# The router of a sparse layer, computed from the unscaled input while the last output tiles still run

## The reference, cut to what matters

```
x = x + gt1 * (mixed @ w_out)
h = rms_norm(x, g_ffn) * (1 + sc2) + sh2
g_logits = h @ w_rg + b_rg                      # 4 groups
e_all    = h @ w_re[g] + b_re                   # 4 experts in each group
g_star = argmax(g_logits);  p_sel = softmax(g_logits)[g_star]
top_v, top_i = top_k(e_all[g_star], 2);  top_w = softmax(top_v) * p_sel
y = sum over the two experts e of  top_w[e] * (silu(h @ w_gate[e]) * (h @ w_up[e])) @ w_down[e]
x = x + gt2 * y
```

## Time and profile before

| what | us |
|---|---|
| three runs: median (lowest to highest) | 2783.74 (2782.13 to 2788.76) |
| the profiled execution, device time | 2782.57 |
| its span, first to last instruction | 2780.7 |
| PE busy, of the span | 2687.7 (97%) |
| DVE busy | 1986.5 (71%) |
| ACT busy | 1456.6 (52%) |
| mean granted TensorE clock, share of full speed | 0.986 |

### The profile page before, as it was taken

One profiled execution on the slowest core, in us unless ns is written; L12 is line 12 of the kernel. 1 busy time (PEld: TensorE's weight loads), 2 busy tenths in 40 slices (PEclk: granted clock), 3 DMA queues, 4 the chain that ended last, 5 costly groups with the idle time before them and its releaser, 6 DMA issues.

```text
span 2780.7 us, 45770 instructions
## 1 busy us (share of the span) xinstructions
PE 2687.7 (97%) x15906; PEld 2309.6 (83%) x15906; DVE 1986.5 (71%) x2871; ACT 1456.6 (52%) x2187; POOL 122.1 (4%) x72
## 2 busy tenths in 40 slices
PE   5999899998999989999999999999999999999999
PEld 3866678885999867788899987999877888899987
DVE  7854689996898566653699947899555753699954
ACT  3353478885555246753555525555336753455532
POOL 1432111100000000000000000000000000000000
PEclk9999799998999999999999999999999999999999
DMA  7731499993332331123233232332333113323222
GB/s 285 276 136 38 169 349 409 405 374 122 103 105 83 102 144 61 53 76 114 91 107 106 91 108 89 99 100 89 101 103 115 60 62 112 108 92 106 91 97 100
DMA packets 95245, 377.57 MB, mean 136 GB/s; under 512 B 10833, under 2 KB 11105, under 8 KB 92897
## 3 DMA queue, kind: packets, MB, share of 16 engines
q1 hardware_dynamic: 89072, 348.69, 35.7%
q0 software_dynamic: 4608, 16.78, 1.5%
q10 hardware_dynamic: 1456, 10.66, 1.0%
HBM read 363.50 MB, written 16.78 MB: 137 GB/s over the span
## 4 chain that ended last, share of the span: by engine, by line
PE 85%; DVE 6%; issue 5%; ACT 3%; DMA 0%; POOL 0%; SPq 0%; ACTq 0%; POOLq 0%; DVEq 0%
PE pb L1404 16%; PE pb L1406 15%; PE pb L1405 15%; PE pb L1789 10%; PE pb L1791 10%; PE pb L1790 10%; PE pb L1973 1%; PE pb L2005 1%; PE pb L1929 1%; PE pb L1478 1%; ACT SP L1286 1%; DVE hid L2689 1%; PE pb L1657 1%; PE pb L1982 1%; DVE SP L2841 0%
## 5 line engine op out<-in xcount | busy, mean ns | idle before, releaser
L1789 PE MATMUL pb<-bl,g_wh 128*128 128x256 f32 x2464 | 701.9, 285 | 9.7 <-DVE bl L2600 5.7
L1790 PE MATMUL pb<-bh,g_wl 128*128 128x256 f32 x2464 | 697.9, 283 | 0.0
L1791 PE MATMUL pb<-bh,g_wh 128*128 128x256 f32 x2464 | 697.8, 283 | 0.0
L1789 PEld LDWEIGHTS pb<-bl,g_wh 128*128 128x128 f32 x2464 | 473.4, 192 | 14.3 <-issue 8.2
L1790 PEld LDWEIGHTS pb<-bh,g_wl 128*128 128x128 f32 x2464 | 473.5, 192 | 1.6 <-issue 1.4
L1791 PEld LDWEIGHTS pb<-bh,g_wh 128*128 128x128 f32 x2464 | 473.6, 192 | 0.0
L2639 DVE TENSOR_TENSOR w_lo<-raw,w_hi 128x1024 fp32r<-128x1024 f32 x164 | 200.3, 1223 | 201.9 <-ACT w_hi L679 201.1
L1404 PE MATMUL pb<-hl,w_hi 128*128 128x512 f32 (+1 forms) x728 | 304.1, 418 | 20.5 <-DVE hl L2133 9.8
L679 ACT ACTIVATE w_hi<-raw 128x1024 fp32r<-128x1024 f32 x194 | 204.2, 1057 | 190.8 <-PE pb L1406 176.7
L1405 PE MATMUL pb<-hh,w_lo 128*128 128x512 f32 (+1 forms) x728 | 287.1, 394 | 0.0
L1406 PE MATMUL pb<-hh,w_hi 128*128 128x512 f32 (+1 forms) x728 | 286.9, 394 | 0.0
(11 more groups left out here) (450 smaller groups left out, 5355.6 us busy)
## 6 DMA issues: line engine op xcount, KB each, us to landing
raw<-in_wstream SPq DMA_DIRECT2D x220, 512.0 KB, 3.3
m_raw<-in_moe_stream SPq DMA_DIRECT2D x96, 512.0 KB, 6.1
g_own<-in_gu_stream SPq DMA_DIRECT2D x44, 768.0 KB, 4.2
raw<-in_gu_stream SPq DMA_DIRECT2D x44, 768.0 KB, 4.2
m_first<-in_moe_stream SPq DMA_DIRECT2D x48, 512.0 KB, 6.0
hf<-in_moe_stream SPq DMA_DIRECT2D x48, 512.0 KB, 5.2
ada_ring<-in_ada SPq DMA_DIRECT2D x8, 2048.0 KB, 8.1
g_own<-in_gu_stream SPq DMA_DIRECT2D x44, 256.0 KB, 3.1
```

Of the source, the lines that this page charges most:

```text
L1789: pe.matmul(o, lh, rl, start=first and k == 0, stop=False, skip_group_check=True)
L1790: pe.matmul(o, ll, rh, start=False, stop=False, skip_group_check=True)
L1791: m = pe.matmul(o, lh, rh, start=False, stop=k == 3, skip_group_check=True)
```

## The change

Instead of h = x * gain * r + shift, with r the inverse root per token, the changed kernel works with u = x * gain, which needs no r:

- The logits are (u W) * r + (shift W + bias). W lies in the vector constants (`router_w`), the shift's share is formed once, early: DVE multiplies W by the shift (`shifted_w`), PE sums it over the partitions with eight matmuls between two projection tiles of the mixer, DVE adds the bias (`route_add`).
- The last two chunks of the output projection are interleaved: the last but one goes through banks 0 to 5, then each bank gets its last part, and behind bank m (from 3 on) stand four matmuls that add u's tile m-3 to the logits with tokens on the partitions (pb0, 20 columns for each 128 tokens). They are plain float32 matmuls.
- ACT squares each x tile (L857) and makes its u tile (L858); DVE sums the squares (`square_in`) and PE sums them over the partitions with four matmuls of one column. r lies per token (`rs_tok`), 128 x 4.
- The token rows are turned from u. ACT multiplies them by r as it copies them, into `hf` itself; the rows in DRAM lack the shift. It is added for every expert as its rows are split: ACT and DVE do it with one instruction for each 128 columns (eight each instead of two), since the shift is one number per partition and k.
- On DVE the weights (`weights()`) come behind the first selection. For expert 0 a product of its own gives the token index alone (`first_rows`), ahead of the weights; the gather of expert 0 waits for that.
- The chunk that held the router weights is streamed still, with zeros. PE waits for its split ahead of the last eight turns.

```diff
-            stats(1)
-            chunk(C_RT // 2, 1)
-            for k in range(KD):
-                pe.wait_ge(hf_ready, k + 1)
-                ...
-                m = mm3(pb[1][0:20, :], w_hi[1][:, k, 0:20], w_lo[1][:, k, 0:20], hh[:, k, :], hl[:, k, :], ...)
+            def logits(k):
+                pe.wait_ge(hf_ready, k + 1)
+                for tt in range(TT):
+                    m = pe.matmul(pb[0][:, 20 * tt:20 * tt + 20], hf[:, k, tt * P:(tt + 1) * P], router_w[:, k, :], ...)
+                if k == KD - 1:
+                    m.then_inc(lg_tok, 1)
...
+            for i in range(2, NMIX - 2):
+                mix_tile(i, range(KD)).then_inc(w_used, 1)
+            mix_tile(NMIX - 2, range(KD - 2))
+            for m in range(KD):
+                if m >= KD - 2:
+                    ins = mix_tile(NMIX - 2, (m,))
+                    ...
+                ins = mix_tile(NMIX - 1, (m,))
+                ...
+                if m >= 3:
+                    logits(m - 3)
+            for k in range(5, KD - 1):
+                logits(k)
+            pe.wait_ge(sq_sum, KD - 1)
+            for tt in range(TT):
+                m = pe.matmul(pb[1][:, tt:tt + 1], rs[:, tt * P:(tt + 1) * P], ones[:, 0:1], start=True, stop=True)
+            m.then_inc(stat_mm, KD)
+            logits(KD - 1)
+            turn_tokens(0, range(TT))
+            turn_tokens(1, range(2))
             chunk(C_RT // 2, 1)
+            pe.sem_inc(w_used, 1)
+            pe.wait_ge(tok_ready, 2)
+            turn_tokens(1, range(2, TT))
...
+            pe.wait_ge(sel_ready, 1)
+            for tt in range(TT):
+                m = pe.matmul(pb[0][:, P:P + 2], sel[0][:, tt, 0, :], combS[:, tt, 0, 2:4], ...)
+            m.then_inc(tab_mm, 1)
             pe.wait_ge(tok_ready, 2 * TT)
             table(0)
```

```diff
+            pe.wait_ge(mod_ready, 3)
+            for k in range(KD):
+                m = pe.matmul(pb[5][:, 0:20], ones, shifted_w[:, k, :], start=k == 0, stop=k == KD - 1)
+            m.then_inc(consts_or_ov_c_mm, 1)
             for i in range(2):
                 chunk(n + 1, i)
```

```diff
-                    act.activation(gh[:, 4 * n:4 * n + 4, :]..., pb[B_T[n]][:], ACT.Copy).then_inc(gh_ready, 1)
+                    for k in range(4):
+                        ins = act.activation(gh[:, 4 * n + k, :], pb[B_T[n]][:, k * P:(k + 1) * P], ACT.Identity,
+                                             bias=modv[:, 32 + 4 * n + k:33 + 4 * n + k])
...
-                    dve.tensor_tensor(gl[:, 4 * n:4 * n + 4, :]..., pb[B_T[n]][:], gh..., ALU.subtract).then_inc(gl_ready, 1)
+                    for k in range(4 * n, 4 * n + 4):
+                        ins = dve.scalar_tensor_tensor(gl[:, k, :], pb[B_T[n]][:, k % 4 * P:(k % 4 + 1) * P], modv[:, 32 + k:33 + k],
+                                                       gh[:, k, :].bitcast(F32), ALU.add, ALU.subtract)
...
             select(0)
-            select(1, range(2))
+            first_rows()
+            weights()
+            select(1)
             table(0)
-            select(1, range(2, TT))
```

More of the change, by code:

```diff
@@ L107 @@
 SUMMED = tuple({norm_of(0): 0, norm_of(2): 4}.get(n, KD - 1) for n in range(3 * NL))
-ADDS = [sum(max(0, m - 1) for m in SUMMED[:n]) for n in range(3 * NL + 1)]
+ADDS = [KD - 1 + sum(max(0, m - 1) for m in SUMMED[:n]) for n in range(3 * NL + 1)]
 STATS = [3 * KD + sum(KD - m + min(m, 1) for m in SUMMED[:n]) for n in range(3 * NL + 1)]
@@ L844, in _ @@
                 hi(C_WOUT // 2 + 2, s, used=False)
-            his(C_WOUT // 2 + 2, 2)
-            squares(1, lambda k: act.wait_ge(x_ready, k + 1))
-            norm_root(1)
+            for s in range(2):
+                hi(C_WOUT // 2 + 3, s)
+            hi(C_RT // 2, 0)
+            for k in range(KD):
+                act.wait_ge(x_ready, k + 1)
+                if k >= 4:
+                    act.wait_ge(sq_sum, max(1, k - 4))
+                act.activation(x_sq[k % 4], x[:, k, :], ACT.Square).then_inc(sq_ready, 1)
+                act.activation(hf[:, k, :], x[:, k, :], ACT.Copy, scale=gs[:, 1, k:k + 1]).then_inc(hf_ready, 1)
+            act.wait_ge(stat_mm, 2 * KD)
+            act.activation(ln_ms, pb[1][:, 0:TT], ACT.Ln, scale=1.0 / D, bias=V("eps")).then_inc(root_ready, 1)
+            act.wait_ge(root_ready, 2)
+            act.activation(rs_tok, ln_ms, ACT.Exp, scale=-0.5).then_inc(rs_ready, 1)
+            hi(C_RT // 2, 1)
             def m_split(n, c):
@@ L1616, in _, with mix_tile @@
-            pe.wait_ge(hf_ready, KD + 1)
-            for tt in range(TT):
-                m = pe.transpose(pb[1][:, 20 * tt:20 * tt + 20], stemp[0:20, tt * P:(tt + 1) * P], ident[0:20, 0:20])
-            m.then_inc(lg_tok, 1)
-            pe.wait_ge(tok_ready, 1)
-            for k in range(4, KD):
-                m = pe.transpose(pb[2][:, k % 4 * P:(k % 4 + 1) * P], hf[:, k, 3 * P:4 * P], ident)
-            m.then_inc(turn_mm, 1)
+            def mix_tile(i, ms):
+                tile = MIX_ORDER[i]
+                chunk(C_WOUT // 2 + i // 2, i % 2)
+                pe.wait_ge(mix_lo, 2 + GH if tile < NU else max(1, tile - NU - NR + 2))
+                return out_tile(i, ms)
@@ new lines, in logits, with turn_tokens @@
+            def logits(k):
+                pe.wait_ge(hf_ready, k + 1)
+                for tt in range(TT):
+                    m = pe.matmul(pb[0][:, 20 * tt:20 * tt + 20], hf[:, k, tt * P:(tt + 1) * P], router_w[:, k, :],
+                                  start=k == 0 and tt == 0, stop=k == KD - 1, skip_group_check=True)
+                if k == KD - 1:
+                    m.then_inc(lg_tok, 1)
+            def turn_tokens(half, tiles):
+                for tt in tiles:
+                    for k in range(4):
+                        m = pe.transpose(pb[B_TOK[half][tt]][:, k * P:(k + 1) * P], hf[:, 4 * half + k, tt * P:(tt + 1) * P], ident)
+                    m.then_inc(turn_mm, 1)
@@ new lines, in _ @@
+            for k in range(5, KD - 1):
+                logits(k)
+            pe.wait_ge(sq_sum, KD - 1)
+            for tt in range(TT):
+                m = pe.matmul(pb[1][:, tt:tt + 1], rs[:, tt * P:(tt + 1) * P], ones[:, 0:1], start=True, stop=True)
[3 more added lines that the diff above has]
+            turn_tokens(1, range(2))
+            chunk(C_RT // 2, 1)
+            pe.sem_inc(w_used, 1)
+            pe.wait_ge(tok_ready, 2)
@@ L1640, in table @@
                 m.then_inc(tab_mm, 1)
+            pe.wait_ge(sel_ready, 1)
+            for tt in range(TT):
+                m = pe.matmul(pb[0][:, P:P + 2], sel[0][:, tt, 0, :], combS[:, tt, 0, 2:4], start=tt == 0, stop=tt == TT - 1)
+            m.then_inc(tab_mm, 1)
             pe.wait_ge(tok_ready, 2 * TT)
@@ L2433, in table @@
                 dve.tensor_reduce(comb_slot[:, own], tab[:, :, 0:2], AX, ALU.add)
-                dve.tensor_copy(h_idx[:, own], tab[:, :, 2])
+                if g > 0:
+                    dve.tensor_copy(h_idx[:, own], tab[:, :, 2])
                 free = small[:, 208 + e0:208 + e1]
```

186 lines of the change are left out of this document (89 added, 97 removed).

## The result

| kernel | median us | lowest to highest | runs |
|---|---|---|---|
| before | 2784.72 | 2782.13 to 2789.48 | 7 |
| changed | 2798.99 | 2795.83 to 2803.75 | 7 |

What follows compares the result with a forecast made beforehand. PE, busy 97% of the span, was taken as the bound; +1.9 - 12.6 + 4.2 + 0.85 = -5.65 us gave 2776.9 by the profiled execution and 2778.1 by the median, forecast 2777.5 us, range 2773 to 2785.

Steps and rivals of the forecast that it cites:

- 1, projections: Between two projection tiles, eight float32 matmuls for the shift's share of the logits lengthen PE's path: +1.9 us.
- 2, output tiles to routing: From output tiles to the start of routing, logits interleaved with the last chunks let routing start earlier: -12.6 us.
- 3, routing to expert 0: From start of routing to expert 0's first product, mainly weights formed after the first selection: +4.2 us.
- 4, experts: Shift added per expert in eight pieces: hidden behind PE in the loop, +0.85 us at its start.
- the 1.5 us put on for half clock: Before routing, the last two or three logit groups cost double after the clock falls: 0.9 to 2.2 us, taken 1.5.
- The listed items: Routing to expert 0: logit operation 0.28, rank and weights -0.95, index, weights, table and counts +4.05, waits 0.1 and 0.3.
- rival A: Between logits and rank, the clock stays up through the turns: saves 3.8 us, 2773.7 us; chance 0.18.
- a way to be wrong: Before expert 0, a listed sign of error: the gather of expert 0 ends the wait for its turns.
- rival C: In the expert loop DVE becomes the bound: 15 experts each 0.85 us longer, 12.7 us, 2790.2 us; chance 0.07.
- D: At the expert loop's start, a 3.0 us wait drops the clock again: 2.7 us more, 2780.2 us; chance 0.08.
- B: In the output tiles, the clock falls while the last banks are still filled: 4.3 us more, 2781.8 us; chance 0.15.

Runs made afterwards that it cites:

- e1_gap640: Kernel before with one unused tile of 640 bytes per partition behind vec, no instruction changed: 2803.84 us, ratio 1.0067.
- e2_router_top: Changed kernel with the router's weights in a tile of their own above all others, loaded by its own DMA: 2777.94 us, ratio 0.9973 to before.
- e11_rounded: Changed kernel with an unused tile of 384 bytes behind vec, rounding the router weights' 640 bytes up to 1024: 2777.03 us, ratio 0.9971 to before.
- e9_gap256: Kernel before with 256 unused bytes behind vec: 2783.02 us in one execution.
- e6_loop_aligned_before: Kernel before with 64 unused bytes ahead of ysb in the experts' area: 2779.01 us, ratio 0.9980.
- e13_early_split: e5_loop_aligned with ACT's rounding of the last, unused weight chunk moved ahead of its wait for the column sums: 2771.87 us, ratio 0.9947 to before.
- e12_index_with_table: e5_loop_aligned without expert 0's own index product; its index comes out of table 0: 2773.37 us, ratio 0.9955 to before.
- e5_loop_aligned: e2_router_top with 64 unused bytes ahead of ysb in the experts' area: 2770.90 us, ratio 0.9952 to before.
- e8_gap64: Kernel before with 64 unused bytes behind vec: 2791.01 us in one execution.
- e10_gap448: Kernel before with 448 unused bytes behind vec: 2809.02 us in one execution.
- e7_two_pieces: e2_router_top with expert rows split in two pieces of 512 columns as before, leaving out their shift: 2774.27 us, ratio 0.9962 to before.
- e14_loop_start: e13_early_split with DVE's split of expert 1's rows and table 4 ahead of expert 0's hidden-row product: 2769.46 us, ratio 0.9938 to before.

## Why the prediction was wrong, step by step

**The step that failed stands in none of the four terms.** The sum took every duration outside the change as fixed and so put at nothing, without a reason, what the new place of the operands costs; one line of the diff, `("router_w", 20 * KD)` in the list of `vec`, moves the operands of some 4,700 products. 0.0055 us each would be 26 us; 19.7 came through (e1_gap640), 21 to 22 by e2_router_top and e11_rounded against the changed kernel. Where the rest went is open; waits of PE could hide it. With it taken away the changed kernel runs in 2777.9 and 2777.0 us; the forecast was 2777.5. That this is so near is in part luck, since the terms miss to both sides. In the traces without the longer step, differences to the trace of before in us:

| term | forecast | e2_router_top | e11_rounded |
|---|---|---|---|
| 1, projections | +1.9 | +1.4 | +1.5 |
| recurrent stage | 0 | +5.1 | 0.0 |
| 2, output tiles to routing | -12.6 | -14.4 | -14.0 |
| 3, routing to expert 0 | +4.2 | +2.9 | +3.2 |
| 4, experts | +0.85 | +1.8 | +1.2 |
| behind the experts | 0 | +1.9 | +1.3 |

In the last row two kernels without the change, e9_gap256 and e6_loop_aligned_before, show +1.1 and +1.2, so most of it need not be the change's.

The trace of before had the sign in it: its experts' products at 0.233 beside dense ones at 0.227, at the same clock and size. I had both numbers and did not ask why they differ.

The Trainium skill would not let one expect such an effect (SBUF — State Buffer, "Who interferes with whom": TensorE has two independent read ports, one for the moving operand and one for the weights' load, and waits on no one). The runs differ from it, and they decide: the step grows by 2 to 6 ns with nothing else changed, and in the trace of after it is 0.2325 (before: 0.2267) even in the 900 and more steps behind the experts during which DVE, ACT and GpSimd are all idle, so it is TensorE's own two operands. By what mechanism they get in each other's way is open; the runs show only the distance.

**1. The shift's share of the logits, +1.9.** The 16 records take 1.86 us, on PE's path, and the last projection product starts 1.4 and 1.5 us later in e2_router_top and e11_rounded: right to half a microsecond. The rest of the 3.8 us is the longer step, which alone makes 1.8 in e1_gap640.

**2. Output tiles to routing, -12.6.** From the first output product to DVE's first logit operation: 74.71 us before, 61.52 after (310.32 - 248.80), 60.30 in e2_router_top, so -13.2 and -14.4. The order was right: column sums, the last logits, the routing. What was mis-sized are the 1.5 us put on for half clock. The clock fell 4.7 us after the start of the last dense product in the profile of after (0.74 between 308 and 310), 1.4 us ahead of routing, and 5.3 us after it in e2_router_top (0.63 between 306 and 308), 0.2 us ahead; I had taken 2.0 to 4.2. Without the 1.5 the term is -14.1.

**3. Routing to expert 0, +4.2.** 24.73 us before, 28.65 after, 27.65 in e2_router_top: +3.9 and +2.9. The listed items add up to 3.8, of which I made 4.2. The size was about right and its parts were not. I left out the block of DVE by GpSimd (+1.95), took the rank at half clock (1.89 us, it took 1.06, since the clock had come back; see rival A below), and took 1.35 us for the turns ahead of the rank: without the block (e13_early_split) DVE is ready at 308.41 and the rank starts at 308.93, 0.5 us late, and with the block the turns are not what it waits for.

Of the block the Trainium skill says (SBUF — State Buffer, "Who interferes with whom") that a VectorE instruction with two SBUF inputs and a GpSimd instruction that reads SBUF block each other whole; by that the trace agrees, 2.19 us against 0.24. I had written that GpSimd's split ends at S + 3, and had asked only what PE would wait for.

That PE does not wait for the gather was wrong: in the trace of after the gather ends a wait of 0.70 us, and in e12_index_with_table, without the early index, one of 1.29. I named that as a way to be wrong, and it was.

**4. The shift per expert, +0.85 at the loop's start.** On DVE 88 pieces take 23.7 us in 11 experts where 22 took 14.0, 0.88 more per expert; on ACT it is 1.08. Forecast were 0.85 and 1.0. A piece takes 0.269 us on DVE. The section of the Trainium skill that rival C cites (VectorE: DVE Perf Modes, "The TRN2 errata") speaks of instructions that read SBUF; these read PSUM and SBUF together. In the loop the extra work is hidden, as forecast: 18.11 us per expert in every kernel but the aligned ones. The wait at the loop's start is 3.02 us; I had 3.0.

**Rivals.** D came true as well in the trace of after: half clock behind that wait, and PE's first turn of hidden rows comes 7.2 us after the loop's first product instead of 5.7, +1.5; I had 2.7. It came in five of the six traces with a wait over 3 us.

C is refuted by the period, and more sharply by e5_loop_aligned, where DVE's 17.31 us fit into 17.68. B did not happen: 1.00 until 308, behind the last dense product.

A did not happen as told, since the clock fell; but my argument against it, that turns never bring the clock back, was wrong. It came back in the midst of the turns, from 310 on in e2_router_top, 3.4 us after the first of them, and 5.7 us after it in the kernel after. Busy time and clock of e2_router_top, then of the kernel after:

```profile
308.00:310.00 2.00, 2.00 (x11) 2.00 (x11) 1.93 (x3) 0.00 (x0) 1.65 (x1) 0.52 0.00 0
310.00:314.00 4.00, 2.18 (x18) 1.71 (x17) 3.42 (x22) 3.78 (x8) 0.00 (x0) 1.00 0.00 0
```

```profile
312.00:314.00 2.00, 2.00 (x12) 2.00 (x11) 1.79 (x7) 0.16 (x1) 0.69 (x1) 0.50 0.00 0
...
316.00:318.00 2.00, 1.12 (x11) 0.88 (x9) 1.58 (x12) 1.79 (x5) 0.00 (x0) 1.00 0.00 0
```

So the rank ran at full clock, 0.8 us that the sum did not have; this and the block that it did not have either went against each other.

**The recurrent stage, +5.1, is not the change's for certain.** It took 72.6 us in ten of the sixteen traces of this study and 74.3 to 81.9 in six, with the clock down in it; the kernel before with 1024 unused bytes is one of the six. Of the eight traces with the change five are longer, of the eight without it one. The change may make it more likely; so few traces do not settle it, and it stays open.

## What to carry to other kernels

When a change adds or resizes a buffer, compare the mean ns and the start-to-start step of untouched groups before reading anything else, and give an added tile a size that keeps the distance between the stationary and the moving operands at a multiple of 256 bytes; here 384 unused bytes were worth 22 us, over three times what the rewrite itself gained. Where a kernel shows two steps for matmuls of one shape and clock, look at their addresses: 64 bytes took 0.43 us off each expert. And when a wait is shortened, work out what arrives next: here the wait for the gather through DRAM swallowed the block's 1.75 to 1.95 us.

## What the runs showed of the hardware

- In an unbroken row of products at clock 1.00, each with a stationary tile of its own, a matmul with 128x512 moving float32 starts 0.2272 us after the one before it if its moving tile lies a multiple of 256 bytes above the stationary one, 0.2291 at 64 over, 0.2326 at 128, 0.2334 at 192 (e8_gap64, e1_gap640, e10_gap448). For 256 columns a step of 0.120 was only seen at a multiple of 256.
- GpSimd's indirect DMA of an expert's output rows takes 0.98 us of its time in the kernel with two pieces and 4.49 with eight, the shift and the pieces the only difference; with eight pieces and the aligned loop (e5_loop_aligned) it is 6.18. Groups of GpSimd, e7_two_pieces and then e2_router_top:

```profile
L632 POOL DMA_INDIRECT y_rows<-ysb,y_idx x11 | 10.8, 981 | 71.6 <-ACT ysb L911 71.6
```

```profile
L632 POOL DMA_INDIRECT y_rows<-ysb,y_idx x11 | 49.4, 4491 | 71.6 <-ACT ysb L914 71.6
```

  The expert's period is 18.11 us with either, so it costs nothing here; why it takes longer wasn't tried.
- Behind PE's wait at the loop's start the clock fell to 0.50 in five traces (waits of 3.02 to 3.21 us: after, e2_router_top, e5_loop_aligned, e11_rounded, e13_early_split) and stayed up in e12_index_with_table (3.17 us), as it did behind waits of 2.15 to 2.51 us (before, e6_loop_aligned_before, e7_two_pieces, e14_loop_start). The length of the wait alone does not decide it.
